# First stage of a two-block transformer kernel: transfers, square sums, weight order and step sizes rearranged

## The chip, the cores and the metric

One core of one Trainium2 chip. The metric is the device time of one execution in microseconds (us). TensorE does the matrix products, VectorE, ScalarE and GpSimd the element work, SyncE and ScalarE issue transfers.

## The reference

The input x is 512 tokens of 1024 channels. A first block has a state-space layer and an attention layer, a second one a recurrent and a banded attention branch and a feed-forward part. Only the beginning matters here:

```
shift, scale, gate = split(silu(c) @ ada_w + ada_b, 3)
h = x * rsqrt(mean(x*x) + eps) * norm_g * (1 + scale) + shift
zxbcdt = h @ in_w                      # 1024 -> 5152
xbc = silu(causal_conv(xbc part))      # 3072 channels
dt = softplus(dt part + dt_bias)       # 32 step sizes a token
a = dt * -exp(a_log);  acum = cumsum(a) within chunks of 128 tokens
```

Everything behind it (the scan over chunks, the output product, both later mixers, the feed-forward part) is the same in both kernels.

## The kernel before, in words

Activations lie transposed: channels on 128 partitions, 512 tokens along the row, so that x is 8 tiles (k = 0 to 7). Each dense product is made of three fp32r products over the same 512 columns: high activations by high weights, low by high, high by low (lines 684 to 686). "High" is a rounded copy that ScalarE makes (`high`, line 2032), "low" the remainder that VectorE makes (`rest`, line 1289), both for weights and activations. Weights come as a stream of chunks of 2048 words a partition into two buffers in turn (`chunk`, line 487, on SyncE). Chunk 0 holds the 32 columns of the step sizes and 96 others, chunk 1 the conv pair 0 and 1, chunk 2 conv blocks 2 and 3, chunk 3 blocks 4 and 5, chunk 4 the first two gate blocks z. A chunk may be loaded when the chunk two before it has been split.

Each engine's program is written out by hand; the order on each is the order in the text, and generators (`take`, `weave`) interleave streams by fixed ratios.

The first stage computes three things at once:

- The factor R = rsqrt(mean square) of each token. ScalarE squares the 8 tiles (line 2052), VectorE adds them (line 1317), TensorE sums over partitions (line 709), ScalarE takes logarithm and exponential (lines 2039 and 2040).
- silu(c) @ ada_w for scale and shift, in eight pieces of 1 MB (A, line 506), one scale and one shift piece for each pair of k. `piece(i)` (line 720) is sixteen small full-precision passes, ScalarE copies the result (`piece_copy`, line 2080), `fold(i)` (line 712) turns it into a column, and VectorE adds the bias (`ada_out`, line 1269).
- From these the normed tiles. `finish_first(i)` (line 1333) makes tiles 2i and 2i+1: both biases, gain, scaling (line 1237) and the low parts (line 1241). ScalarE makes the high parts between (line 2065).

TensorE's own order (lines 732 to 776) starts with fillers: 8 products with zeros, 12 short ones, and `keep_busy` products between the first pieces. After piece 2 the products with finished tiles fill the room between pieces: `dt` is the step-size block (8 k, three products each), `cv01` the conv pair (8 k, six products each). Then come conv blocks 2 and 3, and between them eight transposes ("tk", line 846) of the step sizes and their cumulative sums, which VectorE's scans (line 1370) deliver, then a select product (line 850). The step sizes need, behind the `dt` block, the bias on VectorE (line 1359) and absolute value, exponential and logarithm on ScalarE (lines 2122 to 2124); ScalarE then loads a table, takes a tanh (line 2241) and reads conv blocks 0 and 1 out of their banks (lines 2183 and 2185). VectorE does the conv's taps (lines 1384 to 1386), the gate multiplication (line 1400) and, from block 2 on, the low parts of the weight chunks (line 1289). Three PSUM banks rotate over the dense blocks. SyncE issues X, pieces A0 and A1, chunks 0 and 1, pieces A2 to A7, then chunk 2, a row c, chunk 3; behind the scans it stores them to scratch, and chunk 4 follows.

Rows of the other vectors (`ada_dot`, line 1255) are spread over VectorE's later work.

Of the kernel before, what the change touches and what calls it, by code (L numbers as in the profile page):

```python
# [14 lines left out]
S = 512  # L15
# [9 lines left out]
def weight_plan():  # L25

    plan = [(("m_in_w", 0, 8, ((5120, 32), (0, 96))), [("dt", 0)])]
# [166 lines left out]
SQ_AT = {"x": 0, "y0": 8, "y1": 12, "y2": 16, "y3": 20, "out": 24, "so": 32, "wo": 48, "fd": 56}  # L194
SA_AT = {"x": 0, "y0": 7, "y1": 10, "y2": 13, "y3": 16, "out": 19, "so": 26, "wo": 40, "fd": 47}
# [6 lines left out]
def program(nc, wstream, astream, tstream, crow, vec, con, masks, xT, pT, rbx, out, scratch, pscr):  # L202
# [35 lines left out]
    AP = [sbt(f"AP{n}", [128, 256], F32, ph) for n in range(2)]  # L238
    ph.close()
# [146 lines left out]
    for i, (spec, blocks) in enumerate(plan):  # L386
        for b in blocks:
            chunk_of[b] = i
            if b[0] not in ("pp", "v"):
                at[b] = len(ring)  # L390
                ring.append(b)
            if b == ("cv", 2):
                at["tk", 0] = len(ring)
                ring.append(("tk", 0))
        if not blocks:
# [14 lines left out]
    def bank_read(kind, idx):  # L410
# [5 lines left out]
        of = {"dt": s_dtx, "cv": s_u, "tk": s_wex, "k": s_kt, "q": s_qt, "sz": s_sz, "hq": s_hq, "hf": s_hfr,  # L416
# [61 lines left out]
    s_zero = sem("s_zero")  # L478
    zeros = R
# [4 lines left out]
    def _(e):  # L484
# [162 lines left out]
    def _(e):  # L647
# [15 lines left out]
        def blocks(i, names, js, ncols, ready, hi, lo, kb0=0, first=True, last=True, in_parts=False):  # L663
# [4 lines left out]
            if in_parts:  # L668
                w.wait_ge(s_hi4, 1)
                w.wait_ge(s_lo4, 1)  # L670
            else:
# [5 lines left out]
            for k in range(kb):  # L677
                if in_parts and k == 4:
# [21 lines left out]
        def both(kind, idx, stage, in_parts=False):  # L700

            yield from blocks(chunk_of[kind, idx], [(kind, idx), (kind, idx + 1)], (0, 1), 256, h_ready(stage), *streams(stage),
                              in_parts=in_parts)
# [53 lines left out]
        piece(3)  # L757
        run(take(cv01, 1))
# [3 lines left out]
        fold(4)  # L762
        piece(5)
        run(take(dt, 1))
        fold(5)
        run(take(dt, 1))
# [6 lines left out]
        run(take(dt, 2))  # L773
        run(take(cv01, 1))
        run(dt)
        run(cv01)

# [60 lines left out]
        run(take(first, 8))  # L838
# [13 lines left out]
        run(take(first, 28))  # L852
# [366 lines left out]
    def _(e):  # L1219
# [83 lines left out]
        e.memset(eps[:, 1:2], EPS * EPS)  # L1303
        own(e.memset(sel[:, :], 0.0))
        e.memset(HL[:, 0, 0:256].bitcast(F32), 0.0).then_inc(s_zero, 1)
# [1481 lines left out]
```

## Time and profile before

| | |
|---|---|
| median of 3 runs | 1542.59 us (1542.34 to 1542.92) |
| profiled execution | 1542.45 us |
| its span, first to last instruction | 1540.5 us |
| TensorE busy | 1523.5 us (99%) |
| VectorE busy | 950.5 us (62%) |
| ScalarE busy | 669.5 us (43%) |
| granted TensorE clock, mean | 1.000 |

PE is TensorE's matrix product, PEld its weight load, DVE VectorE, ACT ScalarE, POOL GpSimd, SP SyncE. In the timeline a row is a start, a duration, engine, line, operation, output and inputs; "x16" is sixteen instructions in one row, and the bracket at its end is the idle time of the engine before it and what ended that. A full-precision (f32) matrix product shows as two passes, each with a weight load. The time of a run is about 2 us longer than its span.

### The profile page before, as it was taken

How to read it: one execution, taken by the hardware profiler on the slowest of the kernel's cores; microseconds unless marked ns; L12 is line 12 of the kernel's file. 1: busy time of each engine (PE TensorE's matmuls, PEld its weight loads, DVE VectorE, ACT ScalarE, POOL GpSimd, SP SyncE). 2: the span in 40 equal slices, each digit the busy share in tenths (PEclk: the TensorE clock that was granted, in tenths of full speed). 3: DMA queues.
4: the chain of work that ended last, by engine and by line, in shares of the span. 5: the costliest groups of instructions: out<-in, count | busy, mean ns of one | idle time of the engine just before them, and what ended most of it. 6: DMA issues, size and time to landing. Idle time of an engine off the chain costs nothing.

```text
span 1540.5 us, 18902 instructions
## 1 busy us (share of the span) xinstructions
PE 1523.5 (99%) x7636; PEld 1210.4 (79%) x7636; DVE 950.5 (62%) x1210; ACT 669.5 (43%) x940; POOL 97.4 (6%) x66
## 2 busy tenths in 40 slices
PE   8999999999999999999999999999999999999998
PEld 5888887778788766678888876678888888888887
DVE  5869898996884766755468447744654443432445
ACT  4656567754432655644222355533432223222232
POOL 0000001011300000023000000000110000000110
PEclk9999999999999999999999999999999999999999
DMA  9344344433792211123212333123232323222223
GB/s 390 110 154 171 137 129 133 149 110 132 260 364 96 78 56 47 36 83 110 85 55 68 97 91 102 60 82 106 82 109 83 109 83 109 82 103 103 89 103 123
DMA packets 47733, 179.83 MB, mean 117 GB/s; under 512 B 3696, under 2 KB 20592, under 8 KB 31776
## 3 DMA queue, kind: packets, MB, share of 16 engines
q1 hardware_dynamic: 30688, 169.54, 30.9%
q10 hardware_dynamic: 16960, 9.09, 2.3%
q8 instruction: 61, 1.00, 0.3%
q14 instruction: 24, 0.20, 0.0%
HBM read 174.33 MB, written 4.29 MB: 116 GB/s over the span
## 4 chain that ended last, share of the span: by engine, by line
PE 92%; DVE 3%; ACT 1%; DMA 1%; issue 1%; SPq 0%; POOL 0%; DVEq 0%; ACTq 0%
PE bank L684 25%; PE bank L686 24%; PE bank L685 24%; PE zz L1055 2%; PE bank L1015 1%; PE zz L1003 1%; DMA A<-astream 1%; PE tt L991 1%; PE bank L933 1%; PE bank L931 1%; PE bank L932 1%; PE tt L826 1%; DVE wlo L1289 1%; PE zz L1139 1%; PE bank L1152 1%
## 5 line engine op out<-in xcount | busy, mean ns | idle before, releaser
L684 PE MATMUL bank<-HH,whi 128*128 128x512 f32 x1352 | 550.0, 407 | 0.3 <-DVE HL L1241 0.3
L686 PE MATMUL bank<-HH,wlo 128*128 128x512 f32 x1352 | 528.0, 391 | 0.0
L685 PE MATMUL bank<-HL,whi 128*128 128x512 f32 x1352 | 527.4, 390 | 0.0
L1289 DVE TENSOR_TENSOR wlo<-raw,whi 128x2048 fp32r<-128x2048 f32 (+2 forms) x120 | 262.6, 2188 | 101.8 <-ACT whi L2032 96.6
L684 PEld LDWEIGHTS bank<-HH,whi 128*128 128x128 f32 x1352 | 254.0, 188 | 66.9 <-issue 19.3
L686 PEld LDWEIGHTS bank<-HH,wlo 128*128 128x128 f32 x1352 | 253.8, 188 | 54.7
L685 PEld LDWEIGHTS bank<-HL,whi 128*128 128x128 f32 x1352 | 254.4, 188 | 48.6 <-issue 2.9
L2032 ACT ACTIVATE whi<-raw 128x2048 fp32r<-128x2048 f32 (+2 forms) x116 | 218.6, 1885 | 136.4 <-PE bank L686 108.6
L2649 POOL TENSOR_TENSOR SRT<-SRT 128x512 f32<-128x512 f32 x47 | 82.0, 1744 | 928.4 <-ACT SRT L2052 927.4
L1650 DVE TENSOR_TENSOR_SCAN W<-W,cc 128x511 f32<-128x511 f32 (+3 forms) x64 | 49.0, 808 | 32.2 <-ACT W L2376 32.2
L686 PE MATMUL bank<-FH,wlo 128*128 128x512 f32 x176 | 68.5, 389 | 0.0
L685 PE MATMUL bank<-FL,whi 128*128 128x512 f32 x176 | 68.5, 389 | 0.0
L684 PE MATMUL bank<-FH,whi 128*128 128x512 f32 x176 | 68.5, 389 | 0.0
L1963 DVE TENSOR_TENSOR pst<-bank,SRT 128x512 f32<-128x512 f32 x22 | 15.1, 692 | 72.0 <-PE bank L686 72.0
L2052 ACT ACTIVATE SRT<-X 128x512 f32<-128x512 f32 x40 | 24.7, 627 | 72.3 <-DVE X L1522 53.3
L1975 DVE SCALAR_TENSOR_TENSOR SRT<-SRT,bank 128x512 f32<-128x512 f32 x22 | 15.1, 688 | 65.0 <-PE bank L686 65.0
L2618 ACT ACTIVATE FH<-SRT 128x512 fp32r<-128x512 f32 x22 | 13.9, 632 | 85.9 <-DVE SRT L1975 85.9
L2614 ACT ACTIVATE SRT<-pst 128x512 f32<-128x512 f32 x22 | 13.9, 632 | 82.4 <-DVE pst L1963 82.4
L2203 ACT ACTIVATE E<-AC,atk 128x128 f32<-128x128 f32 x128 | 39.1, 392 | 4.6 <-DMA AC<-scratch 4.6
L2375 ACT ACTIVATE W<-zz 128x1024 f32<-128x1024 f32 (+3 forms) x32 | 22.6, 705 | 38.6 <-PE bank L1015 32.2
L684 PE MATMUL bank<-WH,whi 128*128 128x512 f32 x96 | 38.6, 402 | 0.0
L684 PEld LDWEIGHTS bank<-FH,whi 128*128 128x128 f32 x176 | 33.0, 188 | 7.0
(333 smaller groups left out, 2110.5 us busy)
## 6 DMA issues: line engine op xcount, KB each, us to landing
raw<-wstream SPq DMA_DIRECT2D x113, 1024.0 KB, 4.8
aslot<-tstream SPq DMA_DIRECT2D x24, 512.0 KB, 3.6
A<-astream SPq DMA_DIRECT2D x8, 1024.0 KB, 21.1
AC<-scratch ACTq DMA_DIRECT2D x16, 512.0 KB, 5.2
QT<-tstream SPq DMA_DIRECT2D x12, 512.0 KB, 6.7
OZ<-tstream SPq DMA_DIRECT2D x12, 512.0 KB, 7.6
raw<-wstream SPq DMA_DIRECT2D x4, 768.0 KB, 4.2
X<-xT SPq DMA_DIRECT2D x1, 2048.0 KB, 8.5
```

The costliest lines, as they stand in the source:

```text
L684: e.matmul(o, wh[:, k, c], hi[:, kb0 + k, :], start=first and k == 0, stop=False)
L685: e.matmul(o, wh[:, k, c], lo[:, kb0 + k, :], start=False, stop=False)
L686: x = e.matmul(o, wl[:, k, c], hi[:, kb0 + k, :], start=False, stop=last and k == kb - 1)
L826: x = e.matmul(aux[2][o:o + 64, 128 * q:128 * q + 128], XD[u % 2][:, h, :], E[u % 2][:, h, :], start=True, stop=True)
L1055: m = e.matmul(aux[x % 2][:, 128 * h:128 * h + 128], HK[:, h, cs], HQ[:, h, cs], start=True, stop=True)
L1289: x = e.tensor_tensor(wlo[:, i % 2, c], raw[:, i % 2, c], whi[:, i % 2, c].bitcast(F32), ALU.subtract)
L1650: x = e.tensor_tensor_scan(k, k, diag[:, last], 0.0, ALU.mult, ALU.add)
L2032: e.activation(whi[:, i % 2, 0:n], raw[:, i % 2, 0:n], ACT.Copy).then_inc(s_hi, 1)
L2052: e.activation(dst, src, ACT.Square, scale=scale).then_inc(s_sq, 1)
L2203: x = e.activation(E[(u + 1) % 2][:, h, :], AC[:, h, :], ACT.Relu, scale=-1.0, bias=atk[:, cv_, 8 * gv + h:8 * gv + h + 1])
L2375: e.activation(keep(a, S - hi, S), zz[:, :, 0:hi], ACT.Sigmoid, scale=-1.0)
L2649: e.tensor_tensor(acc, acc, tile, ALU.add).then_inc(s_sqa, 1)
```

## The change

- X is loaded in two transfers of four tiles; chunk 1 goes ahead of chunk 0, and chunk 0 holds only the 32 step-size columns (128 KB in place of 512 KB).
- The squares go to eight tiles of their own (six by ScalarE, the first four as soon as the first transfer is there; two by VectorE). TensorE sums them with eight full-precision products against ones, accumulated in one bank, and VectorE's seven additions are gone. The sigmoid of c is made of an exponential, an addition and a reciprocal, all of the table with logarithm and exponential.
- TensorE's fillers become five products with zeros and four others. The conv pair's first k stands ahead of piece 2; the weights of its first k are split in parts of their own.
- The step sizes: high and low weights lie side by side in 64 columns, each k has one product with the high and one with the low activations, 16 in place of 24, the last eight of them behind the conv pair. The two halves of the result are added behind them (ScalarE copies one, VectorE adds it and the bias). The softplus stands behind the reading of conv block 0, the scans behind its taps, and the transposes behind conv block 3.
- `finish_first` makes gain and scaling of a tile behind the scale, ahead of the shift. Buffers, constants and counts are adapted; small constants of the conv are made early.

```diff
-    plan = [(("m_in_w", 0, 8, ((5120, 32), (0, 96))), [("dt", 0)])]
+    plan = [(("m_in_w", 0, 8, ((5120, 32),)), [])]
...
+        if i == 0:
+            done_at.append((s_mv, 9))
...
+    step_raw = raw[:, 0, 0:256].rearrange("p (k n) -> p k n", k=8)
+    in_parts = {1: {0: 1, 2: 2}, 2: {0: 3}}
...
-        e.dma_start(X[:, :, :], xT).then_inc(l_x, 16)
+        e.dma_start(X[:, 0:4, :], xT[:, 0:4, :]).then_inc(l_x0, 16)
+        e.dma_start(X[:, 4:8, :], xT[:, 4:8, :]).then_inc(l_x, 16)
         for i in range(8):
             ada_first(i)
             if i == 1:
+                chunk(1)
                 chunk(0)
-                chunk(1)
         chunk(2)
...
-        dt, cv01 = block("dt", 0, "in", 0, 128), both("cv", 0, "in", True)
-        w.wait_ge(s_zero, 1)
-        for i in range(8):
-            e.matmul(aux[0][:, :], zeros[:, 0:128], zeros[:, :], start=True, stop=True)
-        for i in range(12):
-            w.wait_ge(s_zero, 2)
-            e.matmul(aux[0][:, 0:128], HL[:, 0, 0:128], HL[:, 0, 128:256], start=True, stop=True)
+        def step_sizes(k):
+            w.wait_ge(s_hi, 1)
+            w.wait_ge(s_lo, 1)
+            w.wait_ge(s_rr, 1)
+            h_ready("in")(k)
+            for h in (HH, HL):
+                x = e.matmul(aux[0][0:64, :], flat(dtw[:, k, :, :]), h[:, k, :], start=(k == 0 and h is HH), stop=(k == 7 and h is HL))
+            if k == 7:
+                x.then_inc(s_mv, 1)
         def keep_busy(n):
             w.wait_ge(l_con, 16)
             for i in range(n):
                 e.matmul(bank_of("cv", 1)[:, 0:256], ones, diag[:, 0:256], start=True, stop=True)
+        cv01 = both("cv", 0, "in")
+        w.wait_ge(s_zero, 2)
+        for i in range(5):
+            e.matmul(aux[0][:, :], zeros[:, 0:128], zeros[:, :], start=True, stop=True)
+        for n, k in enumerate((0, 1, 2, 3, 4, 6, 5, 7)):
+            if k < 6:
+                w.wait_ge(s_sq, k + 1)
+            else:
+                w.wait_ge(s_sqa, k - 5)
+            x = e.matmul(aux[0][:, :], ones0, xsq[:, k, :], start=(n == 0), stop=(n == 7))
+        x.then_inc(s_sum, 1)
         piece(0)
+        keep_busy(1)
+        fold(0)
+        piece(1)
+        keep_busy(1)
+        fold(1)
         keep_busy(2)
-        piece(1)
-        keep_busy(2)
-        sum_of("x", aux[0])
-        fold(0)
-        fold(1)
-        keep_busy(3)
+        run(take(cv01, 1))
         piece(2)
-        run(take(dt, 2))
+        run(take(cv01, 1))
         fold(2)
         piece(3)
-        run(take(cv01, 1))
+        step_sizes(0)
         fold(3)
         piece(4)
         run(take(cv01, 1))
         fold(4)
+        run(take(cv01, 1))
         piece(5)
-        run(take(dt, 1))
+        step_sizes(1)
         fold(5)
-        run(take(dt, 1))
         piece(6)
         run(take(cv01, 1))
         fold(6)
         piece(7)
         run(take(cv01, 1))
         fold(7)
-        run(take(dt, 2))
-        run(take(cv01, 1))
-        run(dt)
+        step_sizes(2)
+        step_sizes(3)
         run(cv01)
+        for k in range(4, 8):
+            step_sizes(k)
...
         first, chunks = in_proj(0), ssd()
-        run(take(first, 8))
+        run(take(first, 16))
         bank_free("tk", 0)
         bank = bank_of("tk", 0)
...
-        run(take(first, 28))
+        run(take(first, 20))
...
+        e.memset(ones0, 1.0).then_inc(s_zero, 1)
...
+        w.wait_ge(l_x, 16)
+        for k in (6, 7):
+            e.tensor_tensor(xsq[:, k, :], X[:, k, :], X[:, k, :], ALU.mult).then_inc(s_sqa, 1)
         w.wait_ge(l_vec, 16)
         w.wait_ge(s_sg, 1)
-        e.tensor_tensor(cact[:, :], sg[:, :], vcol("c"), ALU.mult).then_inc(s_c, 1)
+        own(e.tensor_scalar(cact[:, :], sg[:, :], 1.0, None, ALU.add))
+        own(e.reciprocal(cact[:, :], cact[:, :]))
+        e.tensor_tensor(cact[:, :], cact[:, :], vcol("c"), ALU.mult).then_inc(s_c, 1)
...
-        for k in range(1, 8):
-            w.wait_ge(s_sq, k + 1)
-            w.wait_ge(s_sqa, k - 1)
-            e.tensor_tensor(SQ, SQ, T[(k - 1) % 3][:, :], ALU.add).then_inc(s_sqa, 1)
...
-        def rest_first_conv():
-            w.wait_ge(l_raw[1], 16)
-            for h in range(2):
-                c = slice(1024 * h, 1024 * h + 1024)
-                w.wait_ge(*((s_hi, 2) if h else (s_hi4, 1)))
-                e.tensor_tensor(wlo[:, 1, c], raw[:, 1, c], whi[:, 1, c].bitcast(F32), ALU.subtract).then_inc(
-                    s_lo if h else s_lo4, 1)
+        def rest_part(i, c0, c1, high, low):
+            c = slice(c0, c1)
+            w.wait_ge(l_raw[i % 2], 16 * (i // 2 + 1))
+            w.wait_ge(*high)
+            e.tensor_tensor(wlo[:, i % 2, c], raw[:, i % 2, c], whi[:, i % 2, c].bitcast(F32), ALU.subtract).then_inc(low, 1)
+        def rest_step_sizes():
+            w.wait_ge(l_raw[0], 16)
+            w.wait_ge(s_hi, 1)
+            e.tensor_tensor(dtw[:, :, 1, :], step_raw, dtw[:, :, 0, :].bitcast(F32), ALU.subtract).then_inc(s_lo, 1)
         def finish_first(i):
             ada_out(2 * i)
-            ada_out(2 * i + 1)
-            w.wait_ge(s_ada, 2 * i + 2)
+            w.wait_ge(s_ada, 2 * i + 1)
             o = VOFF["norm_g"][0] + 2 * i
             gain(G1[:, 2 * i:2 * i + 2], cv[:, o:o + 2], ada[:, 8 + 2 * i:10 + 2 * i], i + 1)
+            w.wait_ge(l_x0, 16)
             w.wait_ge(l_x, 16)
             w.wait_ge(s_rr, 1)
-            for k in (2 * i, 2 * i + 1):
-                normed("in", k, G1[:, 0:8])
+            normed("in", 2 * i, G1[:, 0:8])
+            if i == 0:
+                normed("in", 1, G1[:, 0:8])
+            ada_out(2 * i + 1)
+            if i > 0:
+                normed("in", 2 * i + 1, G1[:, 0:8])
+            w.wait_ge(s_ada, 2 * i + 2)
             low_shifted("in", 2 * i, ada[:, 0:8])
+            if i == 0:
+                rest_part(1, 0, 512, (s_hi4, 1), s_lo4)
             low_shifted("in", 2 * i + 1, ada[:, 0:8])
             if i == 0:
-                rest_first_conv()
-        rest(0)
-        finish_first(0)
-        finish_first(1)
-        finish_first(2)
-        finish_first(3)
...
-        w.wait_ge(s_blk, blk_done("dt", 0))
-        e.tensor_scalar(xb, bank_of("dt", 0)[0:32, :], cv[0:32, VOFF["dtb"][0]:VOFF["dtb"][0] + 1], None,
-                        ALU.add).then_inc(s_dtx, 1)
...
+                rest_part(1, 512, 1024, (s_hi4, 2), s_lo4)
+                rest_step_sizes()
+                rest_part(1, 1024, 2048, (s_hi, 2), s_lo)
+        for i in range(4):
+            finish_first(i)
+        rest_part(2, 0, 1024, (s_hi4, 3), s_lo4)
+        rest_part(2, 1024, 2048, (s_hi, 3), s_lo)
+        w.wait_ge(s_mv, 9)
+        w.wait_ge(s_cp, 9)
+        e.scalar_tensor_tensor(xb, aux[0][0:32, :], cv[0:32, VOFF["dtb"][0]:VOFF["dtb"][0] + 1], dts,
+                               ALU.add, ALU.add).then_inc(s_dtx, 1)
...
+        run(take(first, 8))
+        w.wait_ge(s_dte, 1)
+        w.wait_ge(s_dtx, 1)
+        e.scalar_tensor_tensor(dd, xb, 0.0, dd, ALU.max, ALU.add).then_inc(s_dt, 1)
+        w.wait_ge(s_dt, 1)
...
         run(take(first, 15))
...
+        lnexp()
+        for k in range(6):
+            w.wait_ge(l_x if k > 3 else l_x0, 16)
+            square(X[:, k, :], xsq[:, k, :])
         w.wait_ge(l_vec, 16)
-        e.activation(sg[:, :], vcol("c"), ACT.Sigmoid).then_inc(s_sg, 1)
-        lnexp()
-        w.wait_ge(l_x, 16)
-        for k in range(8):
-            square_x("x", k)
+        e.activation(sg[:, :], vcol("c"), ACT.Exp, scale=-1.0).then_inc(s_sg, 1)
...
-        piece_copy(0)
...
-        piece_copy(1)
-        high(0)
         w.wait_ge(s_sum, 1)
         rsqrt(aux[0][:, :], D, R[:, :]).then_inc(s_rr, 1)
-        def high_first_conv(h):
-            w.wait_ge(l_raw[1], 16)
-            c = slice(1024 * h, 1024 * h + 1024)
-            e.activation(whi[:, 1, c], raw[:, 1, c], ACT.Copy).then_inc(s_hi if h else s_hi4, 1)
+        piece_copy(0)
+        piece_copy(1)
+        def high_part(i, c0, c1, high):
+            c = slice(c0, c1)
+            w.wait_ge(l_raw[i % 2], 16 * (i // 2 + 1))
+            e.activation(whi[:, i % 2, c], raw[:, i % 2, c], ACT.Copy).then_inc(high, 1)
         for i in range(4):
             for k in (2 * i, 2 * i + 1):
+                w.wait_ge(s_ada, 2 * i + 2)
                 high_shifted("in", k, ada[:, 0:8])
+                if i == 0:
+                    high_part(1, 512 * k, 512 * k + 512, s_hi4)
             if i == 0:
-                high_first_conv(0)
+                w.wait_ge(l_raw[0], 16)
+                e.activation(dtw[:, :, 0, :], step_raw, ACT.Copy).then_inc(s_hi, 1)
+                high_part(1, 1024, 2048, s_hi)
             if i < 3:
                 piece_copy(2 * i + 2)
-                if i == 0:
-                    high_first_conv(1)
                 piece_copy(2 * i + 3)
...
+        high_part(2, 0, 1024, s_hi4)
+        high_part(2, 1024, 2048, s_hi)
+        w.wait_ge(s_mv, 9)
+        e.activation(dts, aux[0][32:64, :], ACT.Copy).then_inc(s_cp, 1)
...
+        run(take(first, 8))
+        w.wait_ge(s_dtx, 1)
+        w.wait_ge(s_c, 1)
+        e.activation(sg[0:32, 0:1], cv[0:32, VOFF["alog"][0]:VOFF["alog"][0] + 1], ACT.Exp)
+        own(e.activation(dd, xb, ACT.Abs))
+        own(e.activation(dd, dd, ACT.Exp, scale=-1.0))
+        e.activation(dd, dd, ACT.Ln, bias=1.0).then_inc(s_dte, 1)
+        exptanh()
```

## Rows read from the trace of the kernel before

**Rows 1.** The page: span, and the ending chain's shares by engine.

```profile
span 1540.5 us, 18902 instructions
...
PE 92%; DVE 3%; ACT 1%; DMA 1%; issue 1%; SPq 0%; POOL 0%; DVEq 0%; ACTq 0%
```

**Rows 2.** Timeline of TensorE's matrix products: start us, us, engine, line, operation.

```profile
1.46 8.71 PE L736 MATMUL zz<-SRT 128*128 128x512 f32 x16 [1.46 <-DVE SRT L1301]
...
13.03 1.07 PE L727 MATMUL zz<-A,cact 128*32 128x256 f32 x16 [1.57 <-DMA A<-astream]
...
21.77 1.07 PE L727 MATMUL tt<-A,cact 128*32 128x256 f32 x16 [0.80 <-DMA A<-astream]
...
24.27 0.50 PE L717 MATMUL tt<-sel,AP 128*128 128x1 f32 x4
24.70 1.07 PE L727 MATMUL bank<-A,cact 128*32 128x256 f32 x16
25.70 0.50 PE L684 MATMUL bank<-HH,whi 128*128 128x512 f32 x1
...
30.62 0.61 PE L717 MATMUL zz<-sel,AP 128*128 128x1 f32 x4 [0.34 <-ACT AP L2084]
...
43.28 0.47 PE L684 MATMUL bank<-HH,whi 128*128 128x512 f32 x1 [0.34 <-DVE HL L1241]
...
48.86 0.39 PE L684 MATMUL bank<-HH,whi 128*128 128x512 f32 x1
...
60.86 0.40 PE L684 MATMUL bank<-HH,whi 128*128 128x512 f32 x1
```

**Rows 3.** Timeline of ScalarE.

```profile
10.95 3.33 ACT L2052 ACTIVATE SRT<-X 128x512 f32<-128x512 f32 x6
...
18.82 0.69 ACT L2039 ACTIVATE SRT<-zz,eps 128x512 f32<-128x512 f32 x1 [0.55 <-PE zz L709]
...
41.62 1.38 ACT L2065 ACTIVATE HH<-SRT,ada 128x512 fp32r<-128x512 f32 x2 [2.99 <-DVE SRT L1237]
...
46.08 0.62 ACT L2122 ACTIVATE EA<-YT 32x512 f32<-32x512 f32 x1
...
49.34 1.06 ACT L2241 ACTIVATE E<-cbc 128x1024 f32<-128x1024 f32 x1
50.92 0.60 ACT L2183 ACTIVATE U<-bank 128x512 f32<-128x512 f32 x1 [0.52 <-DVE w3h L1377]
...
52.08 0.60 ACT L2183 ACTIVATE U<-bank 128x512 f32<-128x512 f32 x1
```

**Rows 4.** Timeline of VectorE.

```profile
40.14 0.16 DVE L1275 TENSOR_TENSOR ada<-bank,cv 128x2 f32<-128x2 f32 x1 [2.76 <-PE bank L717]
...
42.38 1.42 DVE L1241 SCALAR_TENSOR_TENSOR HL<-SRT,ada,HH 128x512 fp32r<-128x512 f32 x2
...
55.52 0.74 DVE L1384 SCALAR_TENSOR_TENSOR SRT<-U,cv,SRT 128x512 f32<-128x512 f32 x1
...
58.35 2.29 DVE L1289 TENSOR_TENSOR wlo<-raw,whi 128x2048 fp32r<-128x2048 f32 x1
...
81.79 0.69 DVE L1400 SCALAR_TENSOR_TENSOR XS<-SRT 128x512 f32<-128x512 f32 x1
```

**Rows 5.** Timeline of TensorE's weight loads, warm-up products.

```profile
3.33 0.33 PEld L736 LDWEIGHTS zz<-SRT 128*128 128x128 f32 x1 [0.52 <-issue]
4.18 0.33 PEld L736 LDWEIGHTS zz<-SRT 128*128 128x128 f32 x1 [0.52 <-issue]
```

**Rows 6.** Transfers: KB each and us to landing; the pieces' issues.

```profile
X<-xT SPq DMA_DIRECT2D x1, 2048.0 KB, 8.5
...
L506 SPq DMA_DIRECT2D A<-astream x8: 415/470/3408, 1.2 to 9.0; - x8
...
A<-astream SPq DMA_DIRECT2D x1, 1024.0 KB, 26.0
```

**Rows 7.** Stretch 20 to 30 us: PE, PEld, DVE, ACT, POOL busy, PEclk, DMA, GB/s.

```profile
20.00:30.00 10.00, 9.20 (x79) 6.11 (x77) 7.33 (x12) 5.18 (x9) 0.00 (x0) 1.00 1.01 420
```

More of the change, by code:

```diff
@@ L391, in program @@
                 ring.append(b)
[L392 removed]
+            if b == ("cv", 3):
                 at["tk", 0] = len(ring)
                 ring.append(("tk", 0))
[L395 removed]
+        if i == 0:
+            done_at.append((s_mv, 9))
+        elif not blocks:
             n_part += 1
@@ L661, in bank_free, with blocks @@
                 w.wait_ge(read, v)
-        def blocks(i, names, js, ncols, ready, hi, lo, kb0=0, first=True, last=True, in_parts=False):
+        def blocks(i, names, js, ncols, ready, hi, lo, kb0=0, first=True, last=True):
             kb = plan[i][0][2]
@@ L667, in blocks @@
             wl = wlo[:, i % 2, 0:kb * ncols].rearrange("p (k n) -> p k n", k=kb)
[L668 to L671, printed above, removed]
+            parts = in_parts.get(i, {})
+            if i not in in_parts:
                 w.wait_ge(s_hi, i + 1)
@@ L677, in blocks @@
             for k in range(kb):
-                if in_parts and k == 4:
+                if k in parts:
+                    w.wait_ge(s_hi4, parts[k])
+                    w.wait_ge(s_lo4, parts[k])
+                if k == 4:
                     w.wait_ge(s_hi, i + 1)
@@ L698, in block, with both @@
                               h_ready(stage), *streams(stage))
-        def both(kind, idx, stage, in_parts=False):
-            yield from blocks(chunk_of[kind, idx], [(kind, idx), (kind, idx + 1)], (0, 1), 256, h_ready(stage), *streams(stage),
-                              in_parts=in_parts)
+        def both(kind, idx, stage):
+            yield from blocks(chunk_of[kind, idx], [(kind, idx), (kind, idx + 1)], (0, 1), 256, h_ready(stage), *streams(stage))
         def sum_of(name, bank, acc=SQ, n=7):
@@ L1361, in _ @@
-        w.wait_ge(s_hi, 3)
-        e.tensor_tensor(wlo[:, 0, 0:1024], raw[:, 0, 0:1024], whi[:, 0, 0:1024].bitcast(F32), ALU.subtract).then_inc(s_lo, 1)
-        w.wait_ge(s_dte, 1)
-        w.wait_ge(s_dtx, 1)
-        e.scalar_tensor_tensor(dd, xb, 0.0, dd, ALU.max, ALU.add).then_inc(s_dt, 1)
-        w.wait_ge(s_dt, 1)
-        own(e.tensor_scalar(xb, dd, sg[0:32, 0:1], -1.0, ALU.mult, ALU.mult))
-        w.wait_ge(l_con, 16)
-        for c in range(4):
-            x = e.tensor_tensor_scan(ac[:, 128 * c:128 * c + 128], ones[0:32, :], xb[:, 128 * c:128 * c + 128], 0.0,
-                                     ALU.mult, ALU.add)
@@ L1497, in _ @@
         first, chunks = in_proj(0), ssd()
+        run(take(first, 8))
[3 more added lines that the diff above has]
+        w.wait_ge(s_dt, 1)
+        own(e.tensor_scalar(xb, dd, sg[0:32, 0:1], -1.0, ALU.mult, ALU.mult))
+        w.wait_ge(l_con, 16)
+        for c in range(4):
+            x = e.tensor_tensor_scan(ac[:, 128 * c:128 * c + 128], ones[0:32, :], xb[:, 128 * c:128 * c + 128], 0.0,
+                                     ALU.mult, ALU.add)
+        x.then_inc(s_acm, 1)
         run(take(first, 15))
@@ L1508, in _ @@
         e.scalar_tensor_tensor(cbc[:, :], flat(E[1][:, :, :]), 1.0, cbc[:, :], ALU.add, ALU.mult).then_inc(s_cc, 1)
-        weave((take(first, 28), 28), (ada_blocks(0, 3), 12))
+        weave((take(first, 20), 20), (ada_blocks(0, 3), 12))
         weave((first, 24), (take(chunks, 4), 4), (ada_blocks(3, 4), 4))
@@ L2246, in _ @@
         load_ac(0)
-        run(take(first, 28))
+        run(take(first, 20))
         weave((first, 24), (take(chunks, 4), 4))
```

38 lines of the change are left out of this document (13 added, 25 removed).

## The prediction

> **What bounds the kernel now.** First I read the chain that ended last: 92% of the span is TensorE and 1% is data transfer [rows 1]. So only three things count: TensorE work taken away, TensorE standing still, and work of others that makes it stand still. Then I read TensorE in order of time through the first stage [rows 2]. It waits for data before pieces 0 and 2 (1.57 and 0.80 us), and from piece 2 at 21.77 us it is nearly without a gap; the group of products that starts at 43.28 us after 0.34 us of waiting is the last exception, and the second conv pair starts at 48.86 us. Before 21.77 us the matrix engine mostly runs fillers, so what is put there is nearly free; after it, every product and every wait counts in full. The later kernel moves as one with the end of this stage as long as ScalarE and VectorE keep up, so I read these two as well [rows 3, 4]. VectorE does not have much to spare: the low part of the third weight chunk runs from 58.35 us for 2.29 us, to 60.64 us, and its first product starts at 60.86 us [rows 2, 4]. At the other end, the last gate multiplication before the first transposes of the scan is the second half of the group from 81.79 us.
>
> **Before piece 2.** Sixteen warm-up passes become ten. A full-precision product of 512 columns is two passes; the sixteen took 8.71 us, the first four 0.85 us apart (3.33 to 4.18), leaving about 0.44 us for each other [rows 2, 5]. Ten cost 4 x 0.85 + 6 x 0.43 = 6.0 us; with the second memset ahead of them they start at 1.7 and end at 7.7 us. The twelve short ones go too. Then come eight summing products, 16 passes x 0.43 = 6.9 us, in place of seven additions on VectorE and one product. They need squares. X was issued ahead of the first piece (1.2 us) and landed 8.5 us later, at about 9.25 us [rows 6]. Its first half can land no later than that, and at 420 GB/s [rows 7] up to 2.5 us earlier; I take 6.7 us, since the queue is one and in order. ScalarE makes squares each 0.555 us (3.33 us for six) [rows 3], faster than they are used, and VectorE makes the last two. So the sum is complete at 7.7 + 6.9 = 14.6 us, where logarithm and exponential began at 18.82 us. If the half lands only with the whole, it is 2.1 us later. The sigmoid made of exponential, addition and reciprocal is three small steps that end near 11.3 us; piece 0 lands at 13.03 us, so it costs nothing, and the saved table load was under the wait for X anyway.
>
> From 14.6 us the stage is one serial chain: the factor R (0.69 + 0.63 us) ready at 16.2, copy of piece 0 (256 columns; 512 take 0.62 us, so 0.4), fold 0 at 16.6, 0.43, piece 1 (1.0), a filler (0.5), copy and fold 1 by 19.1, addition of the bias (0.2), high part (0.69), low part (0.7), low part of the first two k of the weights (a quarter of 2.29 us, 0.6) [rows 2 to 4]. The conv pair's k=0 starts at 21.5 us instead of piece 2 at 21.77 us: 0.25 us gained. The weights are there: chunk 0 shrinks by 384 KB, which is 0.94 us at 420 GB/s, and this and the swap bring chunk 1 to about 18 us. All pieces behind it land 0.9 us earlier too. The last piece was issued at 9.0 us and landed 26.0 us later, at 35.0 us [rows 6]; it comes to 34.1 us and is wanted at 39. Transfers are not the bound.
>
> **From there to the stage's end.** Before, from 21.77 to 48.86 us, 27.1 us. The change in it:
> - Products: 8 k x 3 become 16, so 8 go. 24 products stand between 43.28 and 48.86 us, 0.23 us each: 1.85 us less. The new ones have 64 weight columns; bounds are half of 0.23 us and all of it. I take all, since both stream the same 512 columns.
> - One more group of products behind a full-precision one: +0.1 us.
> - Waits. A product of k=2i needs the shift of its pair, so it is behind fold 2i+1: end of fold (0.5), bias 0.2, high part 0.69, low part 0.72 and its signal, in all 1.9 to 2.0 us after the fold's start has let the next piece go [rows 2 to 4]. Before, the chain also held gain and scaling (fold 7 to 43.28 us is 3.3 us), but 12 products covered it. Now k=2, k=4 have only one piece of 1.0 us in front, and k=6 four step-size products (1.0 us). Three waits of 0.9 us, 2.7 us; the waits before were 0.34 us at 43.28 and 0.34 us at the fold of 30.62 us, 0.7 us. So +2.0 us.
>
> Sum: -1.85 + 0.1 + 2.0 - 0.25 = 0.0; I take +0.1 us for the steps rounded down, and the second pair starts at 48.95 us. The saving is eaten by waits that the earlier scaling shortens but that lost their cover.
>
> **Behind the stage.** The step sizes are now the last products, where before their softplus began at 46.08 us, ahead of the stage's end [rows 3]. ScalarE therefore has queued behind its wait for them: the copy of the lower half (0.6), reading conv block 0 (50.92 to 52.08: 1.2), absolute value to table load (46.08 to 49.34: 3.3), the tanh for the other vectors (1.06), and only then block 1 (1.2). That is 7.5 us behind the stage's end with signals. VectorE follows with taps and gate (55.52 to 58.35: 2.8) and the low part of chunk 3 (2.29): 12.8 us. TensorE arrives there after 48 products and the transposes, 12.0 us in the kernel before (48.86 to 60.86) less 0.3 us for the select product, which is now behind: 11.7 us. **A new wait of 1.1 us**. With the select product back in, it stands at +0.1 + 1.1 = +1.2 us. Last, VectorE now does one product with the other vectors' rows (1.2 us) behind the low part of chunk 4 instead of in front of it; the gate ahead of the first transposes (81.79 us, two in 1.3 us) becomes about 1.1 us later while TensorE is already 1.2 us later, so 0 to 0.4 us: I take 0.2. After it VectorE has room. Total: **+1.4 us**.
>
> SyncE: the scratch transfer waits for the scans, now at about 55.5 us, some 5 us later, and chunk 4 is queued behind it. Twice as much, X, landed 8.5 us after its issue [rows 6]; 64 us at the latest is before ScalarE asks for it near 66 us. GpSimd is not touched.
>
> **The clock.** At the start the passes are 0.85 us apart, later 0.43 us [rows 2, 5]: the two levels 1.2 and 2.4 GHz, although the profile's slices show a granted clock of 1.00 throughout [rows 7]. Behind the waits of 1.57 and 0.80 us the piece takes 1.07 us each time, as at 24.70 us without a wait, so waits of this length cost no clock here. The Trainium skill, page "TensorE: Matmul & The Clock Gate", section "Part 1: The HAM clock gate", says that half the clock pulses are the default and that only recent activity releases the other half. It speaks against cutting fillers and putting waits between products; by it rival D below would be the result.
>
> **The rivals.**
> - B, the three waits are covered (k=2, 4, 6 ready in time because fold and copies overlap more than I count): -2.7 us, so +1.4 - 2.7 = -1.3 us, 1541.3 us. For it: the scaling is out of the chain. Against: the low and high parts have 0.7 us each in a row.
> - C, the hole before the first k (19.9 to 21.5 us) closes as well: another -1.6 us, about -2.9, and with the late chain hidden -4.0, 1538.6 us. It needs the sum to be ready before 13 us, which the eight products don't allow.
> - D, slower: TensorE's clock falls to its lower level at the waits before k=2, 4 and 6, where TensorE now stands still within 10 us three times. A fall costs 4 passes x 0.42 = 1.7 us, as the start shows. One gives 1545.7, two 1547.4 us; from the second it is outside what a run can tell from no change. Against: rows of the waits above.
> - E, the first half of X lands with the second, since both share sixteen engines with the vector and constant loads: +2.1 us, 1546.1 us.
>
> **The numbers.** The profiled run took 1542.45 us, a span of 1540.5 us [rows 1] and 1.95 us around it; it is 0.14 us under the median 1542.59 us. The forecast is 1542.59 + 1.4 = 1544.0 us. A measurement of this kernel can tell 0.2%, 3.1 us, from no change: below 1539.5 or above 1545.7 us. Chances: forecast 0.66, B 0.15, C 0.05, D 0.06, E 0.08. Faster: C and 0.02 of B, 0.07. Slower: D, E and 0.01 of the forecast, 0.15. Same: 0.78. The range takes in B and E, and a part of the bound of the step-size products (16 x 0.11 = 1.8 us less, were they half) under B: 1540.8 to 1546.3 us.
>
> **What would show it.** The square sums should end near 14.6 us and conv k=0 start near 21.5 us; three waits of about 0.9 us for the low part before k=2, 4 and 6; the pair and the step sizes done near 49 us; a wait of about 1 us for the low part of the weights before the fifth conv block, near 61 us. I am wrong if the waits for the low part are missing, if TensorE runs through at 61 us, or if passes 0.85 us apart appear behind a wait.

## The result, and the profile after

Slower: 1551.35 us median of 4 runs (1551.10 to 1551.85) beside 1542.70 us of the kernel before on the same chip (4 runs, 1542.34 to 1542.92). The ratio is 1.0057, 95% interval 1.0045 to 1.0068, or 8.65 us. Forecast was +1.4 us, with a range up to 1546.3 us, and the prediction's own bound for slower was 1545.7 us. The profiled execution took 1551.1 us, a span of 1548.9 us.

The page of the changed kernel, to be held against [rows 1]: its span, and the ending chain's shares by engine, where VectorE's share has grown from 3% to 5%.

```profile
span 1548.9 us, 18868 instructions
...
PE 91%; DVE 5%; ACT 2%; issue 1%; DMA 1%; POOL 0%; SPq 0%; DVEq 0%; ACTq 0%
```

TensorE's waits from 16 to 100 us of the changed kernel: waiting line, releaser, us in total, times, longest. In the kernel before, this stretch has waits of 0.80, 0.34 and 0.34 us only [rows 2].

```profile
PE zz L837 <- DVE XS L1421: 4.6, 1, 4.6
PE bank L694 <- DVE HL L1265: 2.9, 3, 1.0
PE bank L694 <- DVE wlo L1359: 1.5, 1, 1.5
PE bank L694 <- issue: 1.1, 1, 1.1
```

The timeline of TensorE's products in the changed kernel, which answers to [rows 2]:

```profile
1.62 5.97 PE L761 MATMUL zz<-SRT 128*128 128x512 f32 x10 [1.62 <-DVE HL L1328]
7.43 7.03 PE L767 MATMUL zz<-xsq,HL 128*128 128x512 f32 x16
14.39 1.07 PE L736 MATMUL zz<-A,cact 128*32 128x256 f32 x16
...
18.81 1.11 PE L756 MATMUL bank<-cc 128*128 128x256 f32 x4
21.46 0.66 PE L694 MATMUL bank<-HH,whi 128*128 128x512 f32 x1 [1.54 <-DVE wlo L1359]
...
23.20 0.63 PE L695 MATMUL bank<-HL,whi 128*128 128x512 f32 x1
23.62 0.63 PE L696 MATMUL bank<-HH,wlo 128*128 128x512 f32 x1
24.18 1.43 PE L736 MATMUL tt<-A,cact 128*32 128x256 f32 x16
25.55 0.50 PE L694 MATMUL bank<-HH,whi 128*128 128x512 f32 x1
...
50.17 0.40 PE L748 MATMUL zz<-HH,dtw 128*64 128x512 f32 x1
50.41 0.39 PE L748 MATMUL zz<-HL,dtw 128*64 128x512 f32 x1
50.63 0.39 PE L694 MATMUL bank<-HH,whi 128*128 128x512 f32 x1
...
63.43 0.47 PE L694 MATMUL bank<-HH,whi 128*128 128x512 f32 x1 [1.12 <-issue]
...
89.97 1.11 PE L837 MATMUL zz<-cc,XS 128*128 128x128 f32 x4 [4.58 <-DVE XS L1421]
90.73 0.78 PE L694 MATMUL bank<-HH,whi 128*128 128x512 f32 x1
...
92.59 0.63 PE L695 MATMUL bank<-HL,whi 128*128 128x512 f32 x1
93.02 0.51 PE L696 MATMUL bank<-HH,wlo 128*128 128x512 f32 x1
93.36 0.40 PE L694 MATMUL bank<-HH,whi 128*128 128x512 f32 x1
```

Two stretches show products 0.42 us apart (23.20 to 23.62, 92.59 to 93.02) that are 0.23 us apart elsewhere: TensorE at its lower clock level. The slices of the changed kernel there (columns as in [rows 7]) have a granted clock under 1.00:

```profile
20.00:25.00 5.00, 3.54 (x14) 2.13 (x18) 4.09 (x6) 2.80 (x5) 0.00 (x0) 0.66 1.01 423
...
90.00:95.00 5.00, 5.00 (x18) 4.17 (x19) 0.62 (x2) 2.81 (x4) 0.00 (x0) 0.68 0.82 315
```

How far the later kernel lies behind the one before, at four marks of TensorE's timeline:

| mark | before | after | behind by |
|---|---|---|---|
| second conv pair starts | 48.86 | 50.63 | 1.77 us |
| fifth conv block starts | 60.86 | 63.43 | 2.57 us |
| last transposes ahead of the first scan chunk | 82.53 | 89.97 | 7.44 us |
| the same of the second chunk | 100.55 | 109.50 | 8.95 us |

Forecast were 0.1, 0.9 and 1.4 us for the first three (the prediction's 1.2 us is 0.9 us at the fifth block's start and 0.3 us for the select product behind it). The wait of 1.12 us ahead of the fifth conv block has no releaser in the profile; VectorE's low part of chunk 3 ends at 63.3 us, 0.1 us ahead of that block:

```profile
61.04 2.29 DVE L1313 TENSOR_TENSOR wlo<-raw,whi 128x2048 fp32r<-128x2048 f32 x1
```

More than half of the loss lies between 63 and 90 us, in one wait of 4.58 us. Its chain is read on VectorE, SyncE and ScalarE of the changed kernel:

```profile
71.56 2.29 DVE L1313 TENSOR_TENSOR wlo<-raw,whi 128x2048 fp32r<-128x2048 f32 x1
...
76.60 1.22 DVE L1284 SCALAR_TENSOR_TENSOR aslot<-aslot,cbc 128x1024 f32<-128x1024 f32 x1
...
85.87 2.29 DVE L1313 TENSOR_TENSOR wlo<-raw,whi 128x2048 fp32r<-128x2048 f32 x1 [3.33 <-issue]
88.08 1.22 DVE L1284 SCALAR_TENSOR_TENSOR aslot<-aslot,cbc 128x1024 f32<-128x1024 f32 x1
...
89.22 0.69 DVE L1421 SCALAR_TENSOR_TENSOR XS<-SRT 128x512 f32<-128x512 f32 x1
```

```profile
77.86 0.33 SPq L511 DMA_DIRECT2D aslot<-tstream  x1
78.28 0.38 SPq L502 DMA_DIRECT2D raw<-wstream  x1
```

```profile
83.87 1.92 ACT L2064 ACTIVATE whi<-raw 128x2048 fp32r<-128x2048 f32 x1 [5.85 <-DMA raw<-wstream]
```

In the kernel before, the first row product stood ahead of the low part of chunk 4 and the issues were these:

```profile
68.27 1.22 DVE L1260 SCALAR_TENSOR_TENSOR aslot<-aslot,cbc 128x1024 f32<-128x1024 f32 x1
```

```profile
69.53 0.33 SPq L503 DMA_DIRECT2D aslot<-tstream  x1
69.95 0.38 SPq L494 DMA_DIRECT2D raw<-wstream  x1
```

SyncE loads the next row into the one slot that the row product reads, so it waits for that product, and chunk 5 is the next in its program. The product is now 8.33 us later (68.27 to 76.60), so chunk 5 is issued at 78.28 in place of 69.95 us. Not all of the 8.33 us is the product's new place: with that place restored chunk 5 is issued at 73.73 us (experiment 6), so 4.55 us are, and the other 3.78 us are VectorE's lateness (its gate block ahead ends 2.0 us later, and the two small products that the row product needs, 0.25 and 1.22 us, now stand behind that block). ScalarE stands 5.85 us waiting for it, VectorE's low part and third row product follow, and the gate multiplication for the transposes is last.

### The profile page after: what moved, and what is told of

The parts are those of the page before. It is cut to its first block, busy times and chain, and to the rows that moved or that the text cites. A ratio compares the mean times of both kernels' runs of the same rounds, so it can differ in the third digit from the quotient of the medians.

```text
span 1548.9 us, 18868 instructions
## 1 busy us (share of the span) xinstructions
PE 1525.5 (98%) x7618; PEld 1208.9 (78%) x7618; DVE 946.5 (61%) x1208; ACT 666.3 (43%) x939; POOL 97.4 (6%) x66
## 4 chain that ended last, share of the span: by engine, by line
PE 91%; DVE 5%; ACT 2%; issue 1%; DMA 1%; POOL 0%; SPq 0%; DVEq 0%; ACTq 0%
PE bank L694 24%; PE bank L696 23%; PE bank L695 23%; PE zz L1079 2%; PE bank L1039 1%; PE zz L1027 1%; DVE wlo L1313 1%; PE tt L1015 1%; PE bank L957 1%; PE bank L955 1%; PE bank L956 1%; PE tt L850 1%; PE zz L1163 1%; PE bank L1176 1%; PE tt L822 1%
## 5 line engine op out<-in xcount | busy, mean ns | idle before, releaser
L2064 ACT ACTIVATE whi<-raw 128x2048 fp32r<-128x2048 f32 (+1 forms) x115 | 217.6, 1892 | 141.5 <-PE bank L696 108.8
L2084 ACT ACTIVATE SRT<-X 128x512 f32<-128x512 f32 x32 | 20.1, 628 | 72.0 <-DVE X L1554 53.3
```

The lines of the kernel that those rows point to most:

```text
L2064: e.activation(whi[:, i % 2, 0:n], raw[:, i % 2, 0:n], ACT.Copy).then_inc(s_hi, 1)
L2084: e.activation(dst, src, ACT.Square, scale=scale).then_inc(s_sq, 1)
```

## The experiments

All times below are medians, and "+x" is the difference to the kernel before, measured in turn with it on the same chip (4 to 24 runs of it in each group, 1542.59 to 1542.70 us). The changed kernel stands at +8.65 us.

**1. The order of SyncE alone.** Chunk 5 is issued ahead of the second row load.

```diff
-        run(take(first, 16))
-        weave((first, 60), (ada_blocks(0, 4, 1, 24), 16))
+        run(take(first, 33))
+        weave((first, 43), (ada_blocks(0, 4, 1, 24), 16))
```

> Edit: on SyncE chunk 5 is issued ahead of the second row load (ada_load(1)), nothing else. Theory Q (the 4.6 us wait of the first scan transposes is SyncE's queue: the row load waits for the row product that the change moved behind the low part of chunk 4, and chunk 5 stands behind it): chunk 5 is issued near 64 us instead of 78.3, the wait before the transposes falls from 4.6 to about 1.4 us (VectorE's own work), and the half-clock stretch behind it (passes 0.43 us apart near 91 us) goes: 1551.35 - 3.2 - 1.7 = about 1546.4 us. Rival V (VectorE has too much work before the gate multiplication): the wait stays above 4 us and the time within 1 us of 1551.

Measured: 1548.80 us (1547.38 to 1549.30), +6.17, ratio 1.0038 [1.0023, 1.0053]. Half of what was expected. Chunk 5 was there in time, but the wait of 4.6 us only fell to 2.6 us. VectorE shows why: the row loads, now behind the chunk, come late themselves, and VectorE waits for them twice.

```profile
81.38 1.23 DVE L1284 SCALAR_TENSOR_TENSOR aslot<-aslot,cbc 128x1024 f32<-128x1024 f32 x1 [1.09 <-DMA aslot<-tstream]
...
85.71 1.23 DVE L1284 SCALAR_TENSOR_TENSOR aslot<-aslot,cbc 128x1024 f32<-128x1024 f32 x1 [0.89 <-DMA aslot<-tstream]
```

The wait of 2.6 us still had products at the lower level behind it (clock 0.66 from 88 to 93 us).

One more thing differs in this profile. TensorE's first stage is the same program as in the changed kernel, and the same wait of 1.54 us stands before the conv pair's first k, but no lower clock follows it here. The products behind it are 0.23 us apart, and from first k to k=2 it takes 8.60 us (22.63 to 31.23), where the changed kernel takes 10.15 us (21.46 to 31.61):

```profile
22.63 0.47 PE L694 MATMUL bank<-HH,whi 128*128 128x512 f32 x1 [1.54 <-DVE wlo L1359]
```

```profile
20.00:25.00 5.00, 3.46 (x28) 2.10 (x27) 3.98 (x7) 3.64 (x6) 0.00 (x0) 1.00 1.01 423
```

**2. The hole before the conv pair's first k.** Three more `keep_busy` products fill it, so that TensorE does not stand still for 1.54 us.

```diff
         fold(1)
-        keep_busy(2)
+        keep_busy(5)
         run(take(cv01, 1))
```

> Edit: 5 in place of 2 filler products ahead of the conv pair's first k, so that the 1.54 us in which TensorE stood still before 21.46 us are nearly full. Theory C (the lower clock from 21.5 to 24.9 us comes of TensorE having been too little busy before it, the hole included): the six products and piece 2 go back to 0.23 us and 1.07 us, 1.7 us less: 1549.6 us. Rival: the low clock comes of the whole lighter start (ten warm-up passes in place of sixteen) and stays; then the time is unchanged or up to 0.3 us longer.

Measured: 1551.27 us (1550.76 to 1551.86), +8.64, ratio 1.0057 [1.0040, 1.0074]: no gain, against the expectation. The first part came as expected. With the wait down to 0.25 us the six products are 0.23 us apart and the slice has a full clock (columns as in [rows 7]); TensorE reached the transposes of the step sizes 1.3 us earlier.

```profile
20.00:25.00 5.00, 4.75 (x32) 3.04 (x32) 4.09 (x6) 3.48 (x7) 0.00 (x0) 1.00 1.01 419
...
88.00:93.00 5.00, 4.18 (x12) 3.51 (x13) 1.36 (x4) 2.80 (x3) 0.00 (x0) 0.50 0.79 280
```

The wait for VectorE's gate did not swallow this: it stayed as long as it was (4.7 us), but VectorE's chain had moved along, and the first transposes start 1.15 us earlier (88.82 in place of 89.97 us). Most of it was lost behind them: in this kernel nine products follow at the lower level, 0.43 us apart, where the changed kernel has six. From the first transposes to the second took 20.28 us, 19.53 in the changed kernel and 18.02 in the one before, so 0.4 us of the gain is left there, and at most 0.1 us in the medians. Why this fall lasted longer was not tested.

**3. Both edits together.**

> Edit: both of the other two. If the two causes are independent, 1546.4 - 1.7 = 1544.7 us. If the second half-clock stretch or the wait before the transposes is hidden by the shift, the sum is missed by 1 us or more.

Measured: 1548.47 us (1548.12 to 1548.98), +5.84, ratio 1.0038 [1.0023, 1.0053]: hardly less than with the first edit alone (+6.17). The wait of 2.6 us and the fall behind it remain, and in the profile of the first edit alone there was no lower clock ahead of k=2 that the filler could have won back.

**4. Cover for the three waits.** On top of the third kernel, conv k and step sizes stand one fold later, so that other products lie between a shift piece and the k that needs it.

```diff
         piece(2)
-        run(take(cv01, 1))
+        step_sizes(0)
         fold(2)
         piece(3)
-        step_sizes(0)
+        run(take(cv01, 1))
         fold(3)
         piece(4)
-        run(take(cv01, 1))
+        step_sizes(1)
         fold(4)
...
```

> Edit: on top of both, TensorE's order in the stage: the conv pair's k=1 to 5 and the step-size products each stand one fold later, so that the shift's chain of 2 us has products in front of it. Theory W (the three waits of 0.96 us are lost cover): they go, the last step-size product is done near 46 us in place of 49, and all of 2.9 us is won: about 1541.8 us, faster than the kernel before. Rival: ScalarE's and VectorE's chain behind the step sizes or the weights' low parts end last anyway, and less than 1 us is won.

Measured: 1546.21 us (1545.50 to 1546.69), +3.58, ratio 1.0022 [1.0012, 1.0031]. The step against the third kernel is 2.26 us, and the three waits for HL (2.9 us) are gone. The absolute time was forecast too low, because the wait of 2.6 us was thought solved; here it is 2.8 us, with a fall behind it.

**5. X in one transfer**, on the changed kernel.

```diff
-        e.dma_start(X[:, 0:4, :], xT[:, 0:4, :]).then_inc(l_x0, 16)
-        e.dma_start(X[:, 4:8, :], xT[:, 4:8, :]).then_inc(l_x, 16)
+        e.dma_start(X[:, :, :], xT).then_inc(l_x, 16)
...
-            w.wait_ge(l_x if k > 3 else l_x0, 16)
+            w.wait_ge(l_x, 16)
```

> Edit, on the changed kernel: X in one transfer again, nothing else. Theory S (from the square sums on, the stage is one serial chain, so TensorE's start matters): the first square sum starts at about 10.6 instead of 7.0 us and piece 0 near 17.5 instead of 14.4 to 15.9, and the time is 1.6 to 3 us longer: about 1553.7 us. Rival: the start is hidden by later transfers; within 0.5 us of 1551.35.

Measured: 1553.07 us (1552.41 to 1554.18), +10.48, ratio 1.0068 [1.0055, 1.0082], 1.8 us more than the changed kernel's +8.65. In the profiled execution (1554.18 us, the longest of the four) piece 0 starts at 16.98 us in place of 14.39 us, and the 2.6 us are still there at the first k (24.05 us) and at the fifth conv block (65.99 us). So the stage is serial from the square sums on. In the changed kernel ScalarE's first squares start at 6.31 us and those of the second half at 9.99 us, here all at 9.24 us: the first half of X does land ahead of the second, and rival E is out.

**6. The first row product ahead of the low part of chunk 4**, on the changed kernel, which undoes only that move.

```diff
-        weave((take(first, 20), 20), (ada_blocks(0, 3), 12))
+        rows = ada_blocks(0, 3)
+        run(take(rows, 4))
+        weave((take(first, 20), 20), (rows, 8))
```

> Edit, on the changed kernel: the first row product stands ahead of the low part of chunk 4 on VectorE, as in the kernel before; SyncE is untouched. Theory Q2 (moving that product behind the low part costs through SyncE, because one slot holds the rows: the load of the next row and chunk 5 behind it wait for the product, and the next row product for its load): chunk 5 is issued near 73.5 us in place of 78.3, no row product waits for its load, the wait before the transposes falls from 4.6 to under 1 us, the half-clock stretch behind it goes: 1551.35 - 3.7 - 1.7 = about 1546 us, and less than issuing chunk 5 ahead gave (1548.8). Rival V (VectorE's own work is too much): the wait stays at 2.6 us or more.

Measured: 1547.15 us (1546.07 to 1547.56), +4.56, ratio 1.0028 [1.0017, 1.0040], 4.1 us less than the changed kernel. One place in VectorE's order is half of the loss. SyncE issues chunk 5 at 73.73 us, the wait before the transposes is 1.1 us, and behind it the clock stays up:

```profile
PE zz L837 <- DVE XS L1421: 1.1, 1, 1.1
```

```profile
73.30 0.33 SPq L511 DMA_DIRECT2D aslot<-tstream  x1
73.73 0.38 SPq L502 DMA_DIRECT2D raw<-wstream  x1
```

```profile
90.00:95.00 5.00, 5.00 (x24) 4.14 (x23) 3.51 (x4) 2.27 (x3) 0.00 (x0) 1.00 0.44 185
```

**7. Four repairs**: the filled hole, the cover, the row product first, and ScalarE's tanh of the other vectors behind the reading of conv blocks 1 and 2. The edit on ScalarE:

```diff
         exptanh()
+        run(take(first, 16))
         w.wait_ge(l_cr, 16)
         e.activation(flat(E[1][:, :, :]), cbc[:, :], ACT.Tanh, scale=0.5).then_inc(s_ct, 1)
-        run(take(first, 28))
+        run(take(first, 12))
```

> Edit, on the changed kernel: TensorE's order with cover and the full filler as in e4_cover, the first row product ahead of the low part, SyncE untouched, and on ScalarE the tanh of the other vectors behind the reading of conv blocks 1 and 2 in place of ahead. If the three causes add: no waits for the shift (-2.8 us), no wait before the transposes and no low clock behind it (-5 us), and the wait of 1.1 us for the low part of chunk 3 gone (-1 us): 1551.35 - 9 = about 1542 us, level with the kernel before. Rival: with TensorE 3 us earlier at the stage's end, VectorE and ScalarE are the bound between 50 and 90 us, and it stays above 1544 us.

Measured: 1542.62 us (1541.89 to 1544.08), +0.03, ratio 1.0002 [0.9993, 1.0011]: level with the kernel before.

**8. Three warm-up products in place of five**, on the seventh kernel.

```diff
-        for i in range(5):
+        for i in range(3):
             e.matmul(aux[0][:, :], zeros[:, 0:128], zeros[:, :], start=True, stop=True)
```

> Edit: as e6_cover_row_tanh, with three warm-up products in place of five. Theory S: the sum's products begin as soon as the first squares are there (6.9 us in place of 7.4 to 8.5), so 0.5 to 1.5 us less than e6_cover_row_tanh. Rival C (fewer warm-up products leave the clock low for longer, passes 0.85 us apart until 8 us or more): as long as e6 or longer.

Measured: 1541.72 us (1541.27 to 1542.63), ratio 0.9995 [0.9986, 1.0003], 0.9 us less. The square sums start at 7.32 us in place of 8.19 us in the two profiled executions. These two do not show where the 0.9 us is won: the transposes start at 82.9 us in both, since TensorE's wait for VectorE's gate grew from 1.1 to 1.5 us, and the profiled execution of this kernel (1542.61 us) is one of the two longest of its 11.

**9. The third row product behind the gate multiplications**, on the eighth kernel.

```diff
-        rows = ada_blocks(0, 3)
+        rows = ada_blocks(0, 2)
         run(take(rows, 4))
-        weave((take(first, 20), 20), (rows, 8))
-        weave((first, 24), (take(chunks, 4), 4), (ada_blocks(3, 4), 4))
+        weave((take(first, 20), 20), (rows, 4))
+        weave((first, 24), (take(chunks, 4), 4), (ada_blocks(2, 4), 8))
```

> The version with all four repairs and three warm-up products, and VectorE's third row product moved behind the two gate multiplications that end before the first transposes of the scan (it goes into VectorE's idle stretch of 3.3 us behind them). In the version before it, that product takes 1.22 us from 80.98 us and the gates follow at 82.12 us; TensorE waits about 1.5 us for them. Theory: VectorE's chain ends that wait, so it shrinks to about 0.3 us, and the time falls by 1.0 to 1.3 us, to about 1540.6, ratio to the kernel before 0.9986. Rival: something behind (the row load and the chunk behind it, now issued some 1.3 us later) takes it back, 1541.7, ratio 0.9995.

Measured: 1540.60 us (1540.22 to 1541.61, 11 runs), ratio 0.9988 [0.9979, 0.9997], 1.1 us less than the eighth kernel and 2.0 us less than the kernel before (24 runs). Between 16 and 100 us TensorE's list of waits is down to these, and the transposes start at 80.83 us, 1.70 us ahead of the kernel before:

```profile
PE bank L694 <- issue: 1.1, 3, 0.4
PE zz L726 <- ACT AP L2120: 0.3, 1, 0.3
```

**10 and 11. Parts undone again**, on the eighth kernel: first the cover, then the row product's place.

> The same version of four repairs with three warm-up products, but TensorE's order of the changed kernel (conv k and step sizes not moved a fold later). Theory: the three waits of 0.96 us for the low part come back whole, and the stage ends 2.3 to 2.9 us later, with nothing behind it that hides this, since VectorE's chain moves with it: about 1544.2, ratio 1.0011. Rival: the chain on ScalarE and VectorE behind the stage starts with the step sizes, whose end moves less than the pair's, so part of it is hidden and the cost is under 1.5 us, 1543.0.

Measured: 1544.41 us (1544.08 to 1545.05), ratio 1.0012 [1.0004, 1.0021], 2.7 us above the eighth kernel. The three waits are back whole:

```profile
PE bank L694 <- DVE HL L1265: 2.9, 3, 1.0
```

> The same version of four repairs with three warm-up products, but the first row product back behind the low part of chunk 4. Theory: the row load and chunk 5 are issued 2.3 us or more later, the wait before the first transposes of the scan grows from 1.5 to about 4 us, and products 0.43 us apart stand behind it: 2.5 us of wait and 1.6 us of clock, about 1545.8, ratio 1.0021. Rival: with the stage 4 us earlier and the tanh later, chunk 5 lands in time anyway, 1542.0, ratio 0.9996.

Measured: 1546.66 us (1546.01 to 1547.30), ratio 1.0027 [1.0016, 1.0037], 4.9 us above the eighth kernel. With everything else repaired, this one place costs more than in the changed kernel:

```profile
PE zz L839 <- DVE XS L1423: 4.5, 1, 4.5
```

```profile
86.00:91.00 5.00, 5.00 (x16) 3.92 (x16) 1.21 (x1) 2.78 (x3) 0.00 (x0) 0.68 0.76 297
```

**12. The tanh back in front of conv block 1**, on the ninth kernel.

> The version with all repairs (1540.6 us, ratio 0.9988), but ScalarE's tanh of the other vectors (1.04 us) again right behind the table load, ahead of the reading of conv block 1. Theory: taps of block 1, gate and the low part of chunk 3 follow it on VectorE, and TensorE, which waits 0.39 us for that low part at 58.24 us, waits 1.0 us longer, 1.4 us, as the prediction had this wait (1.1 us): about 1541.6, ratio 0.9995. Rival: VectorE has other work to do in between (the scans, 2.5 us), so the tanh is hidden and the time stays at 1540.6.

Measured: 1541.40 us (1540.98 to 1541.93), ratio 0.9992 [0.9983, 1.0001], 0.8 us more than the ninth kernel (0.7 us by the differences to the kernel before, as the two were measured on different chips). That is less than the 1.0 us expected. TensorE's wait ahead of the fifth conv block went from 0.4 to 1.1 us, and it is now the longest in its list:

```profile
PE bank L694 <- issue: 1.8, 3, 1.1
```

## Why the prediction was wrong

The sign of its forecast, +1.4 us, was right; its size and its class were not: it held "same" for likely, and the result is slower, outside the range.

- **Before piece 2: right, in part by luck.** Sums done at 14.4 us (forecast 14.6), copies of 256 columns 0.36 us (0.4), first k at 21.46 us (21.5). X landed in halves (experiment 5). But in the seven profiled executions with five warm-up products and X in halves, the sums start anywhere from 7.43 to 8.92 us (forecast 7.7); the changed kernel's is the earliest of them.
- **Products and waits of the stage: right.** The sixteen step-size products are 0.23 us apart, as with 128 weight columns. The three waits are 0.96, 0.96 and 0.98 us (forecast 0.9 each). Their cost is shown from both sides: -2.3 us where they are covered, +2.7 us where the cover is undone.
- **The stage's end: 1.7 us late.** Forecast 48.95, measured 50.63 us. Nearly all of it is the lower clock from 21.46 us: six products each 0.20 us longer, 1.2 us, and piece 2 in 1.43 in place of 1.07 us, 0.36 us. It is rival D's price (1.7 us) at a place where the prediction did not put it. It had excluded a fall by the waits of 1.57 and 0.80 us before pieces 0 and 2 [rows 2], which cost nothing; behind the new wait of 1.54 us before the first k there was one. No profile with this hole filled has the fall (experiments 2 to 4 and 7 to 12); of the four with the hole, the changed kernel and experiments 5 and 6 have it, and experiment 1 has not. So the hole belongs to this fall but is not enough for it, and what decides was not tested. The Trainium skill, page "TensorE: Matmul & The Clock Gate", section "Part 1: The HAM clock gate", says that only recent activity releases the second half of the clock pulses; the rows behind the waits of 1.54 and 4.58 us agree, and the waits of 1.57 us in the kernel before and of 1.54 us in experiment 1 show that the length of the wait alone does not say whether a fall comes.
- **The wait before the fifth conv block: right.** Forecast 1.1, measured 1.12 us. The terms written down add up to 7.5 + 2.8 + 2.29 = 12.6 us, not 12.8, which less 11.7 would have been a wait of 0.9 us; measured from the stage's end to the low part's end are 12.7 us. Experiment 12 shows the tanh as a part of it (0.7 us in the traces).
- **"SyncE" and "behind the stage": the step that failed.** The text had seen that a row product moves behind the low part of chunk 4, and charged 0.2 us for it, on VectorE alone. On SyncE it followed only the scratch transfer and chunk 4. It didn't ask who waits for the row product: the next row load, with chunk 5 behind it. So a wait of 4.58 us, and by the fall of the clock behind it 1.5 us more (19.53 in place of 18.02 us between the transposes of the first two chunks), were missing. Experiment 6 gives 4.1 us back by that one place, and experiment 11 takes 4.9 us by undoing it.

Together, by the marks: 1.77 us by the stage's end (0.1 forecast and about 1.6 of clock); 0.8 more by the fifth block (the wait of 1.12 less the moved select product); 4.9 more by the transposes (the wait of 4.58 and the select product); 1.5 more behind. That is 8.95 us, of which the span shows 8.4.

Rivals B and C are refuted by the waits that are there, E by experiment 5. D was right in its mechanism and nearly in its price (1.7 us a fall; measured 1.56 and 1.5 us), with two falls, and wrong in their place: none came behind the three waits that it named.

With the hole filled, four orders mended and two warm-up products less, the changed kernel is 2.0 us faster than the one before (experiment 9); all these together are worth 10.75 us to it (1551.35 less 1540.60). None of them was tried in the kernel before, so how much of the 2.0 us is the change's own is not shown; that kernel's waits between 16 and 100 us come to 1.5 us in all.

## What to carry to other kernels

When an instruction moves on one engine, list who waits for it, SyncE above all, and then what stands behind that waiter in its program: here the place of one row product of 1.22 us held back a weight chunk by 4.6 us. A wait of TensorE is to be priced with what follows it, since the wait of 4.58 us cost 1.5 us again in clock. A saving ahead of an unmended wait is not lost if the waited-for chain moves along: experiment 4 kept 2.3 us with the wait of 2.8 us still there, and experiment 2 lost its 1.3 us mostly in a longer stretch of low clock, so the next wait's fall has to be looked at before a saving is counted. Row loads with one slot should keep a distance: moving them behind the chunk only changed which of the two came late (experiment 1).

## What the runs showed of the hardware that was not expected

- **The start of the clock differs between executions.** Weight loads of warm-up passes take 0.34 us at the lower level and 0.19 us at the higher. In the changed kernel the first of 0.19 us comes at 4.85 us, in the seventh kernel at 6.04 us, with the same ten warm-up passes from 1.62 us on; over the eight profiled executions with ten passes it lies between 4.85 and 7.63 us:

```profile
4.34 0.27 PEld L761 LDWEIGHTS zz<-SRT 128*128 128x128 f32 x1 [0.52 <-issue]
4.85 0.19 PEld L761 LDWEIGHTS zz<-SRT 128*128 128x128 f32 x1 [0.24 <-issue]
```

```profile
5.20 0.34 PEld L761 LDWEIGHTS zz<-SRT 128*128 128x128 f32 x1 [0.52 <-issue]
6.04 0.19 PEld L761 LDWEIGHTS zz<-SRT 128*128 128x128 f32 x1 [0.51 <-issue]
```

  Here the sums stand directly behind, so the difference reaches piece 0 (14.39 and 15.14 us); in the kernel before, TensorE waited for data there and it was hidden. This may be why the runs of the new versions spread more (2.2 us over the 11 of experiment 7, 0.6 us over 24 of the kernel before).
- **Waits and falls.** No product at the lower level followed the waits of about 1 us before k=2, 4 and 6, nor those of 1.1 and 1.5 us before the transposes (experiments 6 to 8). It followed each wait of 2.6 us and more there. Behind the one of 1.54 us before the first k, ahead of which TensorE had run fillers of 256 columns, it came in three profiled executions (the changed kernel, experiments 5 and 6) and not in the fourth (experiment 1), with the same products in front.
